# Storing the pooling state by channel: four small transposes and a staging copy replaced by element-wise stores

## The reference, cut to what matters

```python
def layer(x, pool_prev, ...):
    h = rmsnorm(x, g_mix)
    proj = h @ w_in
    a = proj[..., :o1]                       # (B, T, 512): input of the pooling branch
    ...
    seq_a = a                                # prompt
    seq_a = jnp.concatenate([pool_prev, a])  # sample
    pa = pool_mixer(seq_a, pos0, w_pool, s_pool)[:, -T:]
    new_pool = seq_a[:, -POOL_STATE:]        # last 15 rows
    ...
    merged = gate_a * (pa @ w_pool_out) + gate_b * (sg @ w_gmlp_out)
    x = x + merged @ w_out
    ...                                      # rmsnorm, SwiGLU FFN, final rmsnorm
```

## Time and profile before

| | |
|---|---|
| median of 3 runs | 766.78 us (766.67 to 767.58) |
| profiled execution: its time | 767.94 us |
| profiled execution: span of its slowest core (core 0) | 766.4 us |
| spans of the 8 cores | 762.0 to 766.4 us |
| TensorE busy on that core | 740.9 us, 97% |
| DVE, ACT, POOL busy | 540.3, 353.3, 110.6 us |

### The profile page before, as it was taken

The page is one execution under the profiler, slowest core; times in us unless marked ns, Lnnn a source line. Parts: engine busy times, 40 slices in busy tenths (PEclk is TensorE's granted clock), DMA queues, the critical chain, the costliest instruction groups (busy, mean ns, idle before and its releaser), DMA issues.

```text
span 766.4 us, 14795 instructions; the slowest of 8 cores (762.0 to 766.4 us)
## 1 busy us (share of the span) xinstructions
PE 740.9 (97%) x4856; PEld 435.2 (57%) x4856; DVE 540.3 (70%) x1166; ACT 353.3 (46%) x753; POOL 110.6 (14%) x185
## 2 busy tenths in 40 slices
PE   6899999999999999999999999999999999999995
PEld 3554555666666655456666664445665666654452
DVE  4788868657666665767578658965577655769986
ACT  4487664455444446675545541001554555532222
POOL 5145111001000011110121001000111000002121
PEclk9999999999999999999999999999999999999998
DMA  9999704015312239763698105860486323004662
GB/s 214 250 253 185 172 4 58 1 15 83 42 30 42 29 57 291 124 160 98 117 189 137 29 15 87 261 216 28 63 129 96 46 40 45 1 1 165 213 232 110
DMA packets 46716, 82.93 MB, mean 108 GB/s; under 512 B 20288, under 2 KB 20416, under 8 KB 46624
## 3 DMA queue, kind: packets, MB, share of 16 engines
q0 software_dynamic: 15984, 29.11, 25.9%
q1 hardware_dynamic: 30222, 52.28, 22.7%
q10 hardware_dynamic: 434, 0.60, 0.2%
HBM read 87.83 MB, written 19.49 MB: 140 GB/s over the span
## 4 chain that ended last, share of the span: by engine, by line
PE 87%; DMA 6%; DVE 3%; issue 2%; ACT 1%; POOL 1%; DVEq 0%; ACTq 0%; POOLq 0%; SPq 0%
PE ps L548 84%; DMA X<-xp 3%; DMA Mr<-wpk 2%; DMA Rg<-wpk 1%; PE ps L1089 1%; PE ps L727 1%; DVE X L580 1%; DVE X L588 1%; ACT junk L569 1%; PE ps L884 0%; ACT Fr L569 0%; POOL rs L695 0%; DVE Pr L588 0%; DVE Fr L580 0%; DVE hT L580 0%
## 5 line engine op out<-in xcount | busy, mean ns | idle before, releaser
L569 ACT ACTIVATE Fr<-ps 128x344 f32<-128x344 f32 (+2 forms) x394 | 179.6, 464 | 197.7 <-PE ps L548 184.8
L580 DVE TENSOR_TENSOR Fr<-Fr,ps 128x344 f32<-128x344 f32 (+2 forms) x366 | 179.4, 508 | 105.0 <-ACT Fr L569 67.7
L548 PE MATMUL ps<-hT,Rg 128*128 128x344 f16 x1440 | 245.6, 309 | 1.1 <-ACT Fr L569 1.0
L548 PE MATMUL ps<-Sx,Rg 128*128 128x344 f16 x1080 | 189.8, 309 | 2.1 <-ACT Fr L569 1.0
L548 PEld LDWEIGHTS ps<-hT,Rg 128*128 128x128 f16 x1440 | 139.3, 98 | 74.4 <-issue 6.6
L548 PEld LDWEIGHTS ps<-Sx,Rg 128*128 128x128 f16 x1080 | 103.5, 98 | 58.7 <-issue 9.5
L580 DVE TENSOR_TENSOR X<-X,ps 128x512 f32<-128x512 f32 (+1 forms) x121 | 80.2, 682 | 26.2 <-PE ps L548 23.8
L569 ACT ACTIVATE Fr<-Fr 128x344 f16<-128x344 f32 x138 | 67.3, 488 | 56.8 <-DVE Fr L580 54.6
L613 POOL DMA_DIRECT2D Rg<-wpk x60 | 32.4, 540 | 373.0 <-PE ps L548 372.6
L548 PE MATMUL ps<-Mr,Pr 128*128 128x512 f16 x352 | 82.6, 379 | 0.7 <-DVE X L580 0.6
L569 ACT ACTIVATE junk<-X 128x1025 f16<-128x1025 f32 (+3 forms) x43 | 44.0, 1022 | 80.9 <-DVE X L580 68.4
(11 more groups left out here) (117 smaller groups left out, 574.4 us busy)
## 6 DMA issues: line engine op xcount, KB each, us to landing
Rg<-wpk POOLq DMA_DIRECT2D x60, 256.0 KB, 4.7
X<-xp SPq DMA_DIRECT2D x22, 512.0 KB, 14.7
X<-xd SPq DMA_DIRECT2D x18, 512.0 KB, 5.1
Mr<-wpk POOLq DMA_DIRECT2D x34, 256.0 KB, 8.9
yp<-X SPq DMA_DIRECT2D x14, 512.0 KB, 2.9
xd<-Pr SPq DMA_DIRECT2D x12, 512.0 KB, 5.6
Pr<-xp SPq DMA_DIRECT2D x10, 512.0 KB, 11.2
xd<-X SPq DMA_DIRECT2D x8, 512.0 KB, 4.4
```

What stands on the lines that cost most here:

```text
L548: ins = e.matmul(out=ap, lhsT=l, rhs=rr, start=(start and i == 0), stop=(stop and i == len(pairs) - 1), skip_group_check=more)
L569: return e.activation(out=P.r(out), in_=P.r(in_), func=func, scale=scale, **kw)
L580: return P.add(eng, lambda e: e.tensor_tensor(out=P.r(out), in0=P.r(a), in1=P.r(b), op=op), reads=[a, b], writes=[out], dur=vdur(n, per), ...
```

## The change

The transposes, the two ACT copies and the two row stores go. In their place the channels' tiles are stored as they lie, by an access pattern that walks HBM with a stride, one f32 at a time: 4 transfers of 128 x 16 elements from `aTs` to row 14 of `nps`, and 4 of 128 x 15 from `halo` to `npp`. All eight are on SP's queue. For `npp`, the last 15 columns are first copied from `AB` to `halo` on DVE, one copy per group. The `nps` stores are held until the load of `('po', 3)` has landed, the `npp` stores until the last `nps` store has landed (`after=`). The planner is told 128 and 120 packets per DMA engine for each transfer, at 50 ns.

```diff
-        def dma(q, out, in_, sem, nbytes, prio, after=(), tr=False):
+        def dma(q, out, in_, sem, nbytes, prio, after=(), tr=False, cols=False):
...
-                return e.dma_start(out=out, in_=in_)
+                return e.dma_start(out=out, in_=in_, allow_slow_non_contiguous=True) if cols else e.dma_start(out=out, in_=in_)
...
-        npp_pt = PT()
...
             if b < 3:
                 vcopy(halo[:, g, :], A[:, 16 + L:32 + L], prio, 16)
             else:
-                def tr(e, ps):
-                    return e.transpose(out=ps[:15, g * 128:(g + 1) * 128], in_=A[:, L + 17:L + 32],
-                                       identity=ident_f)
-                pe_multi(npp_pt, tr, prio, 230.0, [A[:, L + 17:L + 32], ident_f], 1)
+                vcopy(halo[:, g, 0:15], A[:, L + 17:L + 32], prio, 15)
...
             if b == 3:
-                act(nout[:15, :], PV(npp_pt, lambda p: p[:15, :]), AF.Copy, base + 40.0)
-                dma('sp', npp[:, :], nout[:15, :], 'q1', rows(16, 2048), 900)
+                for g in range(4):
+                    dma('sp', npp[:, g * 128:(g + 1) * 128].rearrange("r c -> c r"), halo[:, g, 0:15], 'q1', (120.0, 50.0),
+                        900.0, after=[nstore], cols=True)
             if b == 2:
-                pt = PT()
-
-                def atr(e, p):
-                    ins = None
-                    for g in range(4):
-                        ins = e.transpose(out=p[:NSMP, g * 128:(g + 1) * 128], in_=aTs[:, g, :],
-                                          identity=ident_f)
-                    return ins
-                pe_multi(pt, atr, base + 28.0, 230.0, [aTs[:, :, :], ident_f], 4)
-                act(nout[:NSMP, :], PV(pt, lambda p: p[:NSMP, :]), AF.Copy, base + 28.0)
-                dma('sp', nps[:, 14, :], nout[:NSMP, :], 'q2', rows(16, 2048), 900)
+                for g in range(4):
+                    nstore = dma('sp', nps[:, 14, g * 128:(g + 1) * 128].rearrange("t c -> c t"), aTs[:, g, :], 'q2',
+                                 (128.0, 50.0), 900.0, after=[wd_[('po', 3)]], cols=True)
```

## The result

| | before | after |
|---|---|---|
| median of 7 runs each | 766.78 us (766.27 to 768.34) | 789.89 us (776.17 to 806.91) |
| ratio, undisturbed runs | | 1.0146, 95% interval 1.0117 to 1.0174 |
| profiled execution | 767.94 us | 791.00 us |
| spans of the 8 cores | 762.0 to 766.4 us | 764.7 to 789.4 us |

The kernel became slower, far outside the range of 763.4 to 770.0 us. The ratio (1.46%, some 11 us) rests on the two runs of the changed kernel in which no die lags; as far as the one profiled execution shows, the lag of the others comes from its own stalls, so that the ratio is the low end of the price, and the medians lie 23.1 us apart (789.89 - 766.78). Its executions differ by up to 30.7 us (776.17 to 806.91), and the cores of the profiled one by 24.7 us.

What follows compares the result with a forecast made beforehand. TensorE, busy 97% of the span, was taken as the bound; removed transposes save 0.89 us, ACT, DVE and stores nothing, so 766.78 - 0.89 = 765.9 us (767.05 from the profiled execution), range 763.4 to 770.0 us.

Steps and rivals of the forecast that it cites:

- The step that failed: New stores on SP's queue, about 85 to 159 us: 73 us of transfer, priced at nothing because DMA engines were nearly empty.
- these 9 us: Margin by which the nvs store, landing at 126 us, would precede DVE's write of merged at 134.98 us.
- The price t: DMA time of one 4-byte element in the new stores: 74 ns taken, between ends of 23 and 199 ns.
- Case 4: nvs lands late behind dearer element stores, delaying DVE's merged write and TensorE: about 780 to 821 us; chance 0.12.
- its rule (decides at t = 92 ns): Element price at which nvs would land at 135 us, from 85 + 512 t + 3 = 135.
- the wait for the ring: On SP's queue, X loads drain at about 85 us, then nps stores run to 123 us, ahead of nvs.
- The saving of 0.89 us: TensorE without transposes: 0.45 us for the sample's four plus 4 x 0.11 us for the prompt's, carried through.
- the 0.67 us on DVE: Four added copies to halo at 113 to 126 us, covered by TensorE's ready inputs and DVE's slack from 130 us.
- ACT's two copies: Removed copies of 0.59 and 0.57 us, 1.16 us together, priced at nothing because ACT has slack.
- Cases 2 and 3: Work replanned after 72 us: better plan, 763.1 us, chance 0.20; worse plan with added waits, 768.6 us, chance 0.18.
- The rule against the change: For the new stores: non-contiguous last dimension means one descriptor per element; writes under 512 B cost a read-modify-write; chance 0.12.
- My last sentence before the forecast: Altogether wrong if the stores slowed other transfers, as the Rg loads from 166 us, beyond their engine share; no size.

Runs made afterwards that it cites:

- the one with 8 bytes: Changed kernel, same orders, its 4-byte elements written 8 bytes apart into one small HBM scratch buffer; 900.39 us, no ratio.
- the one with 64: Changed kernel, same orders, each 4-byte element written to its own 64-byte block of an HBM scratch tensor; 774.37 us, ratio 0.9983.
- Experiment 2: Changed kernel with the sample's v rows moved to columns of Mr that merged covers only later, freeing the nvs store; 807.11 us, ratio 1.0142.
- harmless variants: Changed kernel with elements 64 or 512 bytes apart in HBM (0.9983 each) or in contiguous runs (0.9998), or tiles turned on DVE (1.0002).
- experiment 1: Changed kernel, every engine's order kept, but the eight stores write each partition's 16 or 15 values as one contiguous run; 795.44 us, ratio 0.9998.

## Why the prediction was wrong, step by step

- **The step that failed** is "I price the stores at nothing; the cover is the empty DMA engines and these 9 us", with "Nobody waits for `nps<-st` or for the new stores themselves". The engines were nearly empty of data (but for 113 to 126 us, a DMA share of 0.32, which the prediction left out of its cover), but they also bring TensorE its next instructions: nobody waits for the stores, yet TensorE waits for what shares the engines with them, 11.5 us on the slowest core. All four kernels with whole element stores across the rows (the changed one, `nvs` freed, either half alone) stopped at the places of the fetch, and so did the one with 8 bytes (16 of its 24 stops) and, once, the one with 64 (2.10 us); with the same orders and runs of 60 bytes none did.
- **The price t was near, by luck, and did not matter.** I took 74 ns, from a row that averages 16 rows of 2 KB and 16 tiny packets; the mean was 66 ns on core 0 and 74 on core 2. The `nps` stores were to run from 85 to 123 us and the queue's packets do fade at 115 to 125 us. But most elements took 9 ns and a few over 0.5 us, and what waits behind feels the landing, 26.0 us, not the mean. A total of transfer time says when a queue is done, not what a packet that arrives in the middle meets.
- **Case 4** (chance 0.12) happened on four cores of eight, by its mechanism, though on core 2, at 74 ns, its rule (decides at t = 92 ns) says that it should not: `nvs` left SP only at 129.42 us, behind 44.79 us in which SP issued the four `nps` stores and 12.46 us for `nps<-st`, and landed 18.3 us later. I had priced the wait for the ring by element time and the landing at 3 us. Experiment 2 shows that it is not needed for the loss.
- **The saving of 0.89 us** on TensorE, the 0.67 us on DVE and ACT's two copies: the counts are as predicted. 0.9983, 0.9998 and 1.0002 of the harmless variants hold 0.89 us (0.12%) within their intervals as well as nothing; its size stays open.
- **Cases 2 and 3** (another plan) fall: experiment 1 has the new plan, no idle time from 75 to 285 us, and a ratio of 0.9998.
- **The rule against the change.** The Trainium skill, DMA: Bandwidth & Descriptors, Rules for kernel authors, was right in direction: one descriptor for each element, to be avoided. The trace agrees on the number (36257 - 20288 = 15,969 more packets under 512 B). What no row of before could show, and the rule does not part, is the destination: 12 ns into SBUF, 66 ns into HBM. I let it stand as a case of 0.12 because I weighed it as a price per element. My last sentence before the forecast, that I would be wrong altogether if the stores slowed other transfers by more than their share of the engines, names the mechanism; it had no chance of its own.

What stays open: how the price divides between neighbours in HBM and the number of writes; what a fetch waits for ahead of its own packet and behind it; what ACT and DVE lacked where they stood still; and whether the writes of one core would do it, since in every run all eight wrote. That queues q8 and q14 carry instructions is the profile's label; for q8 the stops bear it out, one packet's share apart on different cores, chips and kernels.

## What to carry to other kernels

A transfer that nobody waits for is only free if it leaves the DMA engines passable: count its packets and its landing, not its bytes, and remember that instructions come through the same engines. Don't scatter 4-byte elements close together into HBM; turn the tile on an engine with slack, DVE in 32 x 32 blocks for one, and store runs. When TensorE stops in the middle of a group that has no wait in it, look at the instruction queues in that stretch before looking for a semaphore.

## What the runs showed of the hardware

- A 16 KB packet brought some 256 of TensorE's records. It took 1.06 us in quiet, 9.6 us or more ahead of its use, and up to 8.8 us on core 7 beside element writes to HBM; there TensorE stood still at a packet's first record, for up to 15.99 us in the changed kernel, in the middle of a group of matmuls.
- A 4-byte write from SBUF took 12 ns into SBUF, 35 ns into HBM with 512 B to itself, 66 ns in columns of rows, and 155 ns 8 B apart (means; half of the 4-byte packets in columns of rows took 9 ns or less).
- Transfers of 512 such elements, one at a time, took some 10 us each from issue to issue, though an element took 10 ns.
- After 15 us without work TensorE's granted clock was 0.52 for the next 5 us, and a group of four matmuls took 1.30 instead of 0.75 us.
- DVE turned a 128 x 128 f32 tile in 32 x 32 blocks in 0.31 us.
